# Recurrence keys without a root: the norm enters as the inverse of its square, on the write side only

## The reference

```python
kk = heads(k * k_k)
kk = kk / jnp.maximum(jnp.linalg.norm(kk, axis=-1, keepdims=True), 1e-12)
# per head, per token; the seqs a_t = -kk (read vector) and b_t = kk * a (write vector)
sa = einsum('bhvk,bhk->bhv', state, a_t)
state = state * w_t + sa[..., None] * b_t[:, :, None, :] + v_t[..., None] * k_t[:, :, None, :]
out   = einsum('bhvk,bhk->bhv', state, r_t)
```

## Time and profile before

| | |
|---|---|
| median of 3 runs | 1072.56 us |
| the runs | 1070.73, 1072.56, 1075.52 us |
| span of the profiled execution, first to last instruction | 1067.5 us |
| the profiled execution's own time | not listed apart from its span; the runs lie 3.2 to 8.0 us above the span, the median 5.1 us |
| granted TensorE clock, mean over the span | 0.980 of full |
| chain that ended last, by engine | PE 46%, issue 21%, DVE 12%, POOL 12% |
| recurrence with round -1 | about 64 to 500 us |

### The profile page before, as it was taken

One profiled execution on the slowest core, in us unless ns is written; L12 is line 12 of the kernel. 1 busy time (PEld: TensorE's weight loads), 2 busy tenths in 40 slices (PEclk: granted clock), 3 DMA queues, 4 the chain that ended last, 5 costly groups with the idle time before them and its releaser, 6 DMA issues.

```text
span 1067.5 us, 27421 instructions
## 1 busy us (share of the span) xinstructions
PE 976.5 (91%) x11539; PEld 806.6 (76%) x11539; DVE 687.6 (64%) x937; ACT 467.1 (44%) x571; POOL 367.3 (34%) x218
## 2 busy tenths in 40 slices
PE   1898999999999999899999999799999999999994
PEld 1776777786777677677688888688889888898883
DVE  5735667668747867664221255559778787787877
ACT  0335355346435633335423242374634545445351
POOL 7332511311331131124453454235135052250532
PEclk9998999999999999999999999899999999999997
DMA  9332224224232433432443418114052250432201
GB/s 369 105 97 64 81 83 144 62 83 126 88 81 82 116 91 84 111 97 61 126 133 107 143 57 254 55 45 134 27 156 77 81 157 22 135 98 59 79 1 79
DMA packets 122918, 108.03 MB, mean 101 GB/s; under 512 B 5395, under 2 KB 104641, under 8 KB 122817
## 3 DMA queue, kind: packets, MB, share of 16 engines
q1 hardware_dynamic: 113009, 83.46, 26.0%
q10 hardware_dynamic: 9808, 23.08, 7.1%
HBM read 100.23 MB, written 2.10 MB: 96 GB/s over the span
## 4 chain that ended last, share of the span: by engine, by line
PE 46%; issue 21%; DVE 12%; POOL 12%; DMA 3%; ACT 3%; SPq 1%; ACTq 0%; POOLq 0%; DVEq 0%
PE bank L1822 11%; POOL w_lo L735 10%; PE set L2123 6%; PE bank L2123 5%; PE set L1876 4%; PE set L2222 3%; PE set L1888 2%; PE set L1864 2%; PE bank L1803 2%; DVE Q L1238 1%; PE set L1803 1%; PE bank L2259 1%; DMA ptab<-in_mu_shift_dram 1%; PE set L1900 1%; PE bank L2222 1%
## 5 line engine op out<-in xcount | busy, mean ns | idle before, releaser
L670 POOL TENSOR_TENSOR w_lo<-w_raw,w_hi 128x1024 fp32r<-128x1024 f32 (+2 forms) x75 | 171.1, 2281 | 388.2 <-ACT w_hi L765 379.6
L765 ACT ACTIVATE w_hi<-w_raw 128x1024 fp32r<-128x1024 f32 (+2 forms) x81 | 81.8, 1010 | 107.4 <-PE set L2123 36.1
L2184 PE MATMUL set<-a_hi,w_hi 128*128 128x256 f32 x384 | 109.3, 285 | 8.3 <-DVE res L1579 5.6
L794 ACT ACTIVATE Q<-set 128x1024 f32<-128x1024 f32 x56 | 57.4, 1025 | 135.0 <-PE set L1876 68.9
L1822 PE MATMUL bank<-h_hi,w_hi 128*128 128x512 f32 x256 | 107.8, 421 | 2.8 <-POOL w_lo L670 2.8
L2184 PE MATMUL set<-a_hi,w_lo 128*128 128x256 f32 x384 | 108.3, 282 | 0.0
L2184 PE MATMUL set<-a_lo,w_hi 128*128 128x256 f32 x384 | 108.3, 282 | 0.0
L1119 ACT ACTIVATE w_hi<-w_raw 128x1024 fp32r<-128x1024 f32 x70 | 74.3, 1062 | 77.1 <-PE set L2184 63.0
L1822 PE MATMUL bank<-h_lo,w_hi 128*128 128x512 f32 x256 | 103.5, 404 | 0.0
L1822 PE MATMUL bank<-h_hi,w_lo 128*128 128x512 f32 x256 | 103.1, 403 | 0.4 <-issue 0.4
L1579 DVE SCALAR_TENSOR_TENSOR res<-set,mod,res 128x256 f32<-128x256 f32 x192 | 92.9, 484 | 14.8 <-PE set L2184 2.8
(11 more groups left out here) (360 smaller groups left out, 2293.2 us busy)
## 6 DMA issues: line engine op xcount, KB each, us to landing
w_raw<-in_w_ff_dram SPq DMA_DIRECT2D x64, 512.0 KB, 4.4
w_raw<-in_w_in_dram SPq DMA_DIRECT2D x46, 512.0 KB, 3.9
y<-in_w_ada_dram ACTq DMA_DIRECT2D x20, 512.0 KB, 3.7
ada<-in_w_ada_dram SPq DMA_DIRECT2D x16, 512.0 KB, 9.2
Q<-in_w_ada_dram ACTq DMA_DIRECT2D x12, 512.0 KB, 3.9
w_raw<-in_w_rwkv_up_dram SPq DMA_DIRECT2D x8, 512.0 KB, 3.8
w_raw<-in_w_out_dram SPq DMA_DIRECT2D x8, 512.0 KB, 4.4
xtok<-in_x_dram SPq DMA_DIRECT2D x4, 512.0 KB, 9.4
```

The source lines that it names most:

```text
L670: link(pool.tensor_tensor(part_of(k, w_lo), raw_part(k), part_of(k, w_hi).bitcast(F32), ALU.subtract), "lo_ready")
L765: link(act.activation(part_of(k, w_hi), raw_part(k), ACT.Copy), "hi_ready")
L794: link(act.activation(by_half(tile), psum_flat(set_of(name)), ACT.Copy), "act_kept")
L2184: mm = pe.matmul(to, wx[:, i, columns], a[:, form, i, :], start=OPENS[at] and b == 0 and i == 0 and m == 0, stop=i == 1 and m == 2, skip_g ...
```

## The change

`norm_root` is gone from ScalarE. VectorE waits for TensorE's sums itself, reads them from PSUM, clamps them at 1e-24 and inverts them; it is now VectorE's clamp that counts `norm_taken`. The spread value is one over the norm squared. `t1` (in `keys_over_square`) is the scaled key over the norm squared and goes only into the write vectors, with the sign; the read vectors come from the projected keys `xk` times the column `k_k`. Order and slots of all other instructions stay.

```diff
-            def norm_root(it, q):
-                m = 2 * (it + 1) + q
-                wait_made(act, f"norm{q}", it)
-                if m:
-                    act.wait_ge(sem("inverse_ready"), m)
-                link(act.activation(norms[:, :], pset[set_of(f"norm{q}")][:, 0, 0:2 * TB], ACT.Sqrt), "norm_taken")
...
-                if s == 14 and prep:
-                    norm_root(it, 1)
...
-                if s == 5:
-                    if prep:
-                        norm_root(it, 0)
...
             def norm_inverse(n, q):
-                dve.wait_ge(sem("norm_taken"), 2 * n + q + 1)
-                link(dve.tensor_scalar(norms[:, :], norms[:, :], 1e-12, None, ALU.max))
+
+                wait_made(dve, f"norm{q}", n - 1)
+                link(dve.tensor_scalar(norms[:, :], pset[set_of(f"norm{q}")][:, 0, 0:2 * TB], 1e-12 ** 2, None, ALU.max), "norm_taken")
                 if 2 * n + q:
                     dve.wait_ge(sem("inverse_taken"), 2 * n + q)
                 link(dve.reciprocal(inverse[:, :], norms[:, :]), "inverse_ready")
...
-            def unit_keys(n, q):
+            def keys_over_square(n, q):
...
-                kk, w = (t.rearrange("p (h c t) -> p h c t", h=2, t=C) for t in (t1[:, :], t4[:, q, :]))
+                k, w = (t.rearrange("p (h c t) -> p h c t", h=2, t=C) for t in (xk[:, q, :], t4[:, q, :]))
                 a = one_g(At, q).rearrange("p h (c t) -> p h c t", t=C)
                 for h in range(2):
-                    link(dve.scalar_tensor_tensor(out=a[:, h, :, 1:C], in0=kk[:, h, :, 1:C], scalar=-1.0, in1=w[:, h, :, 0:C - 1],
+                    link(dve.scalar_tensor_tensor(out=a[:, h, :, 1:C], in0=k[:, h, :, 1:C], scalar=col(90 + m), in1=w[:, h, :, 0:C - 1],
                                                   op0=ALU.mult, op1=ALU.mult))
-                link(dve.tensor_scalar(a[:, :, :, 0:1], kk[:, :, :, 0:1], -1.0, None, ALU.mult))
+                link(dve.tensor_scalar(a[:, :, :, 0:1], k[:, :, :, 0:1], col(90 + m), None, ALU.mult))
...
-                link(dve.scalar_tensor_tensor(out=one_g(Bt, q), in0=tokens(a[:, :]), scalar=0.5, in1=tokens(t3[:, :]), op0=ALU.mult, op1=ALU.mult))
+                link(dve.scalar_tensor_tensor(out=one_g(Bt, q), in0=tokens(a[:, :]), scalar=-0.5, in1=tokens(t3[:, :]), op0=ALU.mult, op1=ALU.mult))
```

More of the change, by code:

```diff
@@ L1392, in slot @@
                     if prep:
-                        unit_keys(n, 0)
+                        keys_over_square(n, 0)
                         keys(n, 0)
@@ L1426, in slot @@
                     if prep:
-                        unit_keys(n, 1)
+                        keys_over_square(n, 1)
                     if work:
```

## The result

The change makes the kernel slower: 1093.03 us against 1074.01 (4 runs each), ratio 1.0148, 95% interval 1.0102 to 1.0195. The ratios and intervals here leave out the runs over 1.5% above the fastest of their kernel, and the medians do not: 1102.7 us of the changed kernel (the medians alone would give 1.0177), one of ten with POOL held, four of nine with the pieces ahead. The changed kernel scatters more than the one before, 1084 to 1103 us. The profiled execution took 1089.06 us and spans 1087.3, 19.8 more than before. The forecast was 1079.9 with a range to 1087: the direction was right, the size less than half of the measured one.

What follows compares the result with a forecast made beforehand. TensorE's written order was taken as the bound; gains of 5.6 us (2.0 + 1.6 + 2.0) against 9.7 for D1's stops and 3.2 for the clock gave +7.3, from 1072.56 to 1079.9 us, range 1069 to 1087.

Steps and rivals of the forecast that it cites:

- The set comes free late: Ahead of D1, rounds 0 to 2: TensorE waits for VectorE's later clamp to free norm0's PSUM set; +9.7 us net.
- nothing more would be given back: D1's stops: beyond KR1's vanished waits, later waits recover none of the 9.7 us; full give-back was a rival, chance 0.15.
- The first half of round -1: Without the root, slot 7's landing goes earlier and TensorE's whole 2.00 us wait for POOL's low half goes; 2.0 us gained.
- The second half of round -1: Without the table load, TensorE's stop before the second inverse falls from 2.11 to 0.52 us; 1.6 us gained.
- Round 0, second half: TensorE's 1.95 us stop before 177.52 ends on VectorE's own work, no table load; nothing gained.
- The clock: Half-clock stretches behind TensorE stops: 3.2 us added behind D1's new stops, 2.0 us gained at round -1's second inverse.
- two falls in three: Behind D1's three new stops: two bring a low-clock stretch of 1.6 us each; +3.2 us, bounds 0 and 7.8.
- one that goes: Behind round -1's second inverse: with only 0.5 us of stop the clock's fall most likely goes; -2.0 us, bounds 0 and 2.6.
- The rival in which the clock goes against it throughout: All three D1 stops bring a long low stretch, 7.8, and round -1 keeps its own; +13.9, 1086.5 us; chance 0.10.
- Costs at nothing: VectorE's clamp from PSUM and the read vectors' column product: no added time, hidden by VectorE's spare 20 us a round.

Runs made afterwards that it cites:

- POOL held: Changed kernel, with POOL's low half in slot 14 waiting until VectorE has inverted the second half's norm; 1.0076, 1081.0 us.
- the pieces ahead: Changed kernel, with the projection pieces of slots 6 and 7 emitted on TensorE between A4T and D1; 1.0036, 1078.7 us.
- the stop alone: Kernel before, root and table loads kept, with TensorE waiting ahead of D1 in rounds 0 to 2 for VectorE's first-half clamp; 1.0168, 1093.5 us.
- the kernel with the copy: Changed arithmetic, but ScalarE copies the sums out of PSUM in its old slots, VectorE clamps and inverts from SBUF; 0.9977, 1069.8 us.
- the kernel with the clamp early: Changed kernel, with VectorE's first-half norm inverse moved from slot 6 to slot 4, right behind the decay sums; 1.0013, 1073.3 us.
- the half stop: Kernel before, with TensorE waiting ahead of D1 only until VectorE has copied A4; 1.0043, 1076.7 us.

## Why the prediction was right and wrong

The direction and the mechanism were right, the size was not: +7.3 forecast, +19.0 in the medians, +19.8 between the profiles, about +16 by the ratio 1.0148. The measured 1093.0 us lies outside the range of 1069 to 1087.

*The set comes free late.* The three stops were forecast to within 0.35 us, the absence of one in round 3 too, and the stop alone on the old kernel brings the whole loss. That nothing more would be given back was right in the sum and not place by place: KR0's 0.16 in round 1 went too, and two unexplained stops lost 1.5 and 1.2 us, against others that grew.

*The first half of round -1.* 2.0 us gained, as forecast: by norm1 TensorE was 1.8 us ahead (95.69 for 97.49). The 1.9 at AT1 are not the same 2.0. At the second inverse only 0.5 were left (100.01 for 100.55), and the rest came back behind it, where the low clock lasted 3.4 us instead of 6.8.

*The second half of round -1.* This step failed. "VectorE waited 1.97 us, so it was free at 98.12 and can take the sums at once" took VectorE's instructions at their old durations. But the edit that removes the root also lets ScalarE's high half go 5.6 us earlier (94.43 for 100.02), and POOL's low half with it, onto a VectorE instruction of the same chain. VectorE was free at 99.52. The stop became 3.37 us and not 0.52: 2.9 us mis-sized. Holding POOL shows 2.2 of them, since it brings the stop to 1.20. The other 0.7 can be read from the rows and were not tested. The sum left norm1's end at 98.44 after counting a gain of 2.0 us ahead of it; norm1 ended at 96.64. VectorE, which began this chain 1.9 us earlier than before (86.28 for 88.23), was only 0.8 us earlier at the scaled sum (95.66 for 96.43): the meeting with POOL at 87.07 costs it 1.0 us more than the one at 91.11 did, and the wider products 0.2. The Trainium skill's rule on the shared ports (cited above) pointed to the collision; I had asked what the freed ScalarE gives and not what it sets off.

*Round 0, second half.* "Nothing is gained" was true and incomplete: 2.1 us were lost to the same cause.

*The clock.* +3.2 for two falls in three and -2.0 for one that goes, +1.2 in all; the profile has 20.5 us more at the lower level in the recurrence, some 8 us. This step failed too, in three places. All three of D1's stops brought a fall, 17.0 us of low clock and not two of 3.4. The fall at the second inverse of round -1 did not go, since its stop did not; it was half as long as before (3.4 for 6.8 us), some 1.3 us by the price above and not 2.0. And 13.7 us of low clock came in round 3, 5.3 us of time, which no term held and which the second profile of the same kernel does not have; a like one, 13.7 us from 455, stands in the kernel with the copy, which has no stop at D1. That this fall follows from the change is not shown. The reading of the kernel before was short as well: it named falls after 100.55 and 157.18 and missed those at 130 (behind a wait of 1.49 us), 178 and 314. The rival in which the clock goes against it throughout had the mechanism and stopped at 1086.5, since it did not hold the longer stops at the inverses. These two terms, 5.0 for the inverses and 7 for the clock, make 12 of the 12.5 us between forecast and profile; the clock's part rests on the price of 0.39, and its agreement is partly luck, as the falls differ from one execution to the next.

*Costs at nothing.* The clamp from PSUM takes 0.17 us as before. The products with a column in place of a number take 0.50 us for 0.44 each, the short one 0.23 for 0.17; hidden, but for the 0.2 us in the second half of round -1.

## What to carry to other kernels

A semaphore that hands on a value may also free a buffer: when its producer is moved to another engine, read off who writes the buffer next, and what stands before the new producer in its engine's order. An engine that is relieved starts what it feeds earlier; look at whether that lands on an instruction of the critical chain. A stop in a stream of matmuls cost about twice its length here when it was 3 to 4 us long (1.2 to 2.8 times by the interval), and the lower clock accounts for up to half of that, by the estimate above. A gain that is counted ahead of a wait moves every time in that wait: carry it along before sizing the next term.

## What the runs showed of the hardware

- A VectorE instruction on SBUF and a GpSimd one that starts 0.02 to 0.20 us before it did not share: VectorE's took 2.60 for 0.43 us, 3.22 for 1.28 and 2.92 for 0.69, GpSimd's 3.45 for 2.35 the other way round. VectorE's `TENSOR_SCALAR` that started 0.09 us ahead of GpSimd's lost even so (2.78 for 0.55 us, in eight of the traces).
- Within one kernel the time tends to follow the granted clock of the run: the kernel before had 1066.4 us at 0.983 and 1077.4 at 0.969, the changed one 1084.1 at 0.977 and 1102.7 at 0.950. The slope over 32 runs of the kernel before is 0.20 us per microsecond at the lower level, less than the 0.39 of the recurrence's round 3; over three other groups of its runs (25, 17 and 17) it is 0.17, 0.06 and 0.25. Part of the low time costs nothing: the kernel with the clamp early had 17 us of it at 27 to 45 us, where the kernel before had none, and its first norm stands at 81.1 us for 81.0.
- Stops of 1.5 to 2.5 us were followed by half the clock at some places (behind 100.55, 130.37, 157.18 and 177.52 in the kernel before, 465.54 in the changed one) and not at others (87.86 and 452.87 in the kernel before). The 2.00 us stop at 87.86 stands in the kernels with the stop alone and the half stop too, and there 3.4 us of half clock follow it.
- A table load cost 1283 ns wherever it stood, and no drain beside it showed.
